# Sample sequences' state products interleaved with the output projection of one step

## What is computed

```python
def _gla_chunk(S, q, k, v, g):
    b = jnp.cumsum(g, axis=2)
    b_last = b[:, :, -1, :]
    o_inter = jnp.einsum('nhld,nhde->nhle', q * jnp.exp(b), S)
    ...
    o_intra = jnp.einsum('nhij,nhje->nhie', scores, v)
    k_dec = k * jnp.exp(b_last[:, :, None, :] - b)
    S_new = jnp.exp(b_last)[..., None] * S + jnp.einsum('nhld,nhle->nhde', k_dec, v)
    return S_new, o_inter + o_intra

def _layer(x, p, S0, conv_prefix, lw):
    h = _rmsnorm(x, lw['g_mix_pre'])
    proj = h @ lw['w_in']
    ...
    mix = jnp.concatenate([o, s_out], axis=-1) @ lw['w_out']
    x = x + _rmsnorm(mix, lw['g_mix_post'])
    ...
```

## Time and profile before

| | us |
|---|---|
| median of 3 runs | 2683.9 |
| lowest and highest run | 2680.67, 2685.6 |
| profiled execution | 2687.82 |
| its span in the trace | 2686.1 |
| PE busy in the span | 2605.3 (97%) |
| DVE, ACT, POOL busy | 1042.8, 878.9, 494.4 |
| mean granted clock of PE | 0.979 |

### The profile page before, as it was taken

The page is one execution under the profiler, slowest core; times in us unless marked ns, Lnnn a source line. Parts: engine busy times, 40 slices in busy tenths (PEclk is TensorE's granted clock), DMA queues, the critical chain, the costliest instruction groups (busy, mean ns, idle before and its releaser), DMA issues. The chain is left out here.

```text
span 2686.1 us, 36949 instructions
## 1 busy us (share of the span) xinstructions
PE 2605.3 (97%) x13668; PEld 2340.0 (87%) x13668; DVE 1042.8 (39%) x1721; ACT 878.9 (33%) x1796; POOL 494.4 (18%) x608
## 2 busy tenths in 40 slices
PE   8999999889999999999999999999899999999998
PEld 6789899768777899999999999999688878887887
DVE  4200000277884644444444444443511243334332
ACT  4311111243553533333333333333412142233322
POOL 1100100144654111111111111111000013231222
PEclk9999999878999999999999999999899999999999
DMA  5211222453344311111111111112644486653221
GB/s 169 86 63 61 71 71 66 130 155 108 109 134 142 124 54 41 53 40 54 38 57 38 57 37 58 35 57 74 186 112 107 112 246 174 197 155 116 70 88 44
DMA packets 269574, 254.35 MB, mean 95 GB/s; under 512 B 22792, under 2 KB 229356, under 8 KB 269452
## 3 DMA queue, kind: packets, MB, share of 16 engines
q1 hardware_dynamic: 269490, 253.24, 30.9%
HBM read 176.73 MB, written 76.46 MB: 94 GB/s over the span
## 5 line engine op out<-in xcount | busy, mean ns | idle before, releaser
L2132 PE MATMUL up_acc<-xh,up_wh 128*128 128x416 f32 x1760 | 619.6, 352 | 0.0
L2132 PE MATMUL up_acc<-xl,up_wh 128*128 128x416 f32 x1760 | 616.5, 350 | 0.0
L2132 PE MATMUL up_acc<-xh,up_wl 128*128 128x416 f32 x1760 | 616.1, 350 | 0.0
L2063 DVE SCALAR_TENSOR_TENSOR up_conv<-up_up,ffn_features,up_conv 128x416 f32<-128x416 f32 (+1 forms) x440 | 284.0, 646 | 570.1 <-ACT up_conv L1985 557.9
L2132 PEld LDWEIGHTS up_acc<-xh,up_wl 128*128 128x128 f32 x1760 | 330.1, 188 | 4.2
L2132 PEld LDWEIGHTS up_acc<-xl,up_wh 128*128 128x128 f32 x1760 | 330.8, 188 | 2.8
L2132 PEld LDWEIGHTS up_acc<-xh,up_wh 128*128 128x128 f32 x1760 | 329.9, 187 | 2.9
L1979 ACT ACTIVATE up_up<-up_acc 128x416 f32<-128x416 f32 (+1 forms) x220 | 113.0, 514 | 606.5 <-PE up_acc L2132 606.5
L2665 PE MATMUL down_acc<-ple_wh,ple_sh 128*128 128x512 f32 x704 | 276.8, 393 | 16.0 <-DVE ple_wl L2487 11.4
L2665 PE MATMUL down_acc<-ple_wl,ple_sh 128*128 128x512 f32 x704 | 276.2, 392 | 0.0
L2665 PE MATMUL down_acc<-ple_wh,ple_sl 128*128 128x512 f32 x704 | 275.8, 392 | 0.0
(11 more groups left out here) (337 smaller groups left out, 4234.4 us busy)
## 6 DMA issues: line engine op xcount, KB each, us to landing
lanes<-hidden SPq DMA_DIRECT2D x31, 1408.0 KB, 7.5
hidden<-up_conv SPq DMA_DIRECT2D x110, 208.0 KB, 1.9
up_raw<-in_w_up SPq DMA_DIRECT2D x44, 512.0 KB, 3.9
proj_features<-in_outs SPq DMA_DIRECT2D x60, 208.0 KB, 1.9
up_x_area<-in_w_down SPq DMA_DIRECT2D x40, 256.0 KB, 5.5
in_raw<-in_w_in SPq DMA_DIRECT2D x17, 512.0 KB, 4.0
in_x<-in_x_prompt SPq DMA_DIRECT2D x16, 512.0 KB, 3.6
mix_ru<-proj_features SPq DMA_DIRECT2D x16, 512.0 KB, 5.5
```

Of the source, the lines that this page charges most:

```text
L2063: last = nc.vector.scalar_tensor_tensor(out=out, in0=x(c), in1=out, scalar=taps[:, at, c:c + 1].rearrange("p a c -> p (a c)"), op0=ALU.mul ...
L2132: last = nc.tensor.matmul(acc[b][:, 0:TB], w[kind][:, k, :], x[:, k, b * TB:(b + 1) * TB], start=(k == 0 and p == 0), stop=(k == KC - 1 an ...
```

## The change

The 36 sample products of `sample_outputs` in step 6 are no longer issued in a row ahead of `make_kv(6)`. They keep their order and are issued one or two at a time (one after the first product, two after the second, and so on) behind the 24 products of half 1 of `project(4, 1)`. The waits stay ahead of the first of them. `mix_crossed(6)` still stands between the two pieces of half 1. `s_outputs` is signalled by the last sample product, now behind the last product of half 1.

```diff
-            def project(o, h, chunks):
+            def project(o, h, chunks, beside=None):
...
                     for p, (xx, ww) in enumerate(((sh, wh), (sh, wl), (sl, wh))):
                         last = nc.tensor.matmul(acc_of(o)[h][:, :], xx[s][:, k, :], ww[:, k, 512 * h:512 * h + 512],
                                                 start=(k == 0 and p == 0), stop=(k == KC - 1 and p == 2))
+                        if beside is not None:
+                            beside(k * 3 + p)
                 if k == KC - 1:
                     last.then_inc(summed, 1)
...
-            def sample_outputs():
-                pe.wait_ge(s_masked, 2)
-                pe.wait_ge(s_k_copied, 2)
-                pe.wait_ge(s_state_in, 32)
-                pe.wait_ge(s_v_in, 32)
-                for q in range(2):
-                    for f in range(2):
-                        h = 2 * q + f
-                        nc.tensor.matmul(s_o[f][:, q * TS:(q + 1) * TS], x.v[head_rows(f), h * DV:(h + 1) * DV],
-                                         x.scores[head_rows(f), q, :], start=True, stop=False)
-                        for b in range(SEQS):
-                            cols = slice(b * SL, (b + 1) * SL)
-                            last = nc.tensor.matmul(s_o[f][:, q * TS + b * SL:q * TS + (b + 1) * SL],
-                                                    x.state[head_rows(f), b, q, :], x.q_state[head_rows(f), q, cols],
-                                                    start=False, stop=(b == SEQS - 1))
-                last.then_inc(s_outputs, 1)
+            def sample_output(i):
+                q, f, b = i // 18, i // 9 % 2, i % 9 - 1
+                h = 2 * q + f
+                if i == 0:
+                    pe.wait_ge(s_masked, 2)
+                    pe.wait_ge(s_k_copied, 2)
+                    pe.wait_ge(s_state_in, 32)
+                    pe.wait_ge(s_v_in, 32)
+                if b < 0:
+                    nc.tensor.matmul(s_o[f][:, q * TS:(q + 1) * TS], x.v[head_rows(f), h * DV:(h + 1) * DV],
+                                     x.scores[head_rows(f), q, :], start=True, stop=False)
+                else:
+                    cols = slice(b * SL, (b + 1) * SL)
+                    last = nc.tensor.matmul(s_o[f][:, q * TS + b * SL:q * TS + (b + 1) * SL],
+                                            x.state[head_rows(f), b, q, :], x.q_state[head_rows(f), q, cols],
+                                            start=False, stop=(b == SEQS - 1))
+                    if i == 35:
+                        last.then_inc(s_outputs, 1)
+
+            def sample_outputs_beside(j):
+                for i in range(j * 3 // 2, (j + 1) * 3 // 2):
+                    sample_output(i)
...
                 if t == SB + 4:
                     sample_positions()
-                    sample_outputs()
...
                 if projects(t - 2):
-                    project(t - 2, 1, range(0, 4))
+                    project(t - 2, 1, range(0, 4), sample_outputs_beside if t == SB + 4 else None)
                 if mixes(t):
                     mix_crossed(t)
                 if projects(t - 2):
-                    project(t - 2, 1, range(4, KC))
+                    project(t - 2, 1, range(4, KC), sample_outputs_beside if t == SB + 4 else None)
```

## The result

The changed kernel is slower: 2701.67 us (median of 4 runs, 2697.98 to 2704.51) against 2683.3 of the kernel before on the same chip (4 runs, 2680.67 to 2685.6). The ratio is 1.0067, with an interval of 1.0055 to 1.008. On the medians that is +18.4 us; the forecast was +18.9.

The account below looks back on a forecast made before the run. PE, busy 97% of the span, was taken to bound the kernel. Step 6 +14.4, step 7's opening +2.0 and project(5, 0) +2.5 made +18.9 us, on the 2683.9 median 2703; range 2697 to 2708, low end widened to 2686.

Parts of the forecast that it names:

- The trips: Half 1 of step 6: 24 switches between 128-row and 64-row products expose weight loads, 0.3 us each at full clock, 0.43 at half.
- loads hide: Rival: in half 1 first passes load weights under the running product, no trip cost, clock holds; 2677 us, chance 0.07.
- the wait: End of step 6: mix_last waits for advance(6, 0), behind sample_copies on DVE, which waits for the last sample product; 1.3 us.
- The clock: Half 1: about 4 us at full clock, then 0.50 until some us into project(5, 0), about 40 us instead of 17.
- Step 6: Whole step after the change: 11.1 + 33 + 2.0 + 1.3 = 47.4 us against 33.0, +14.4.
- Up to half 1: Part of step 6 ahead of half 1: 11.1 us at full clock, with 1.1 of sample_positions.
- the groups: Half 1: one product, three passes on average and a trip take 0.87 us at full clock, 1.50 at half.
- Behind it: After step 6: step 7's slow opening +2.0 us and project(5, 0) at half clock +2.5.
- The opening: Step 7's first small products: 2.3 us before, about 4.3 at half clock, +2.0.
- The recovery: Start of project(5, 0) in step 7: runs at half clock until full clock is granted again, +2.5 us.
- `scale_rows(4)`: Step 7, ahead of project(5, 0): DVE is late, 5.8 us, but PE is ready only after 7.0 at half clock; no cost.
- Later steps move as a block: Steps after step 7 stay bound by PE as before and only shift, adding nothing.

Follow-up runs that it names:

- third experiment: Changed kernel with each of the 24 projection products of half 1 issued three times ahead of its sample products; 2698.88 us, ratio 1.0053 to the kernel before.
- the version with both heads: Changed kernel with both heads in one 128-row sample product, 20 products instead of 36, behind most of half 1's first 18 products; 2675.21 us, ratio 0.9974.
- the two kernels with both heads in a row: The both-heads version with its 20 products in a row behind sample_positions, 2677.03 us; and that with sample_state moved to the end of step 6, 2676.43 us.
- second and third experiment: Second: changed kernel with sample products of 128 rows instead of 64, padded with zeros, same places; 2683.44 us, ratio 1.0001. The third experiment has its own line.

## Why the prediction was right

**The trips.** The loads don't start under the products when the row count changes: 0.3 us per group at full clock, as forecast (0.86 in the third experiment against 0.87), and gone with the same row count (0.57). The rival "loads hide" is out for 64 rows. For 128 rows its mechanism is there, but not its price: the rival let the first pass of a group go free (0.23 + 2 x 0.11 = 0.45), and with the load hidden the group still takes 0.57. The Trainium skill (TensorEngine Tiling (Array Packing), "Key Properties") says that a change of the tiling mode drains TensorE; that is the rule that spoke against this change, and the loads at 659.20 and 660.87 agree with it. The rule behind the rival (weight loads are pulled ahead) held here only where the number of rows stayed. At half clock the trip was sized a little too high: 0.38 for the 0.43 assumed, so half the clock makes a trip only about a quarter dearer (0.30 at full clock). By these numbers, as an estimate, the 24 trips are 9 of the 14.7 us of step 6, the wait 1.3, and what is left is mainly the longer half clock.

**The clock.** Forecast: about 4 us at full clock in half 1, then 0.50 to some us into project(5, 0), about 40 us. Measured: 2.7 us, then 41.0. The reason given, too little projection in PE's stream, is supported by two comparisons. The 128-row kernels with 1.5 and with 2 sample products per group differ only in density (a product once in 0.57 or in 0.68 us); the first held 1.00 through half 1, the second fell to 0.50, in one profiled execution each. The stronger one is three products per trip, with the 64-row passes and all trips in place: it holds the clock through half 1 where one product per trip does not, and the means of all eight runs agree. From 652.97 to the wait of 1.32 ahead of 685.84 PE was busy all the time, at 0.50, so the absence of gaps did not save the clock.

**Step 6.** 47.7 against 47.4. Up to half 1 650.29 - 639.17 = 11.1 (11.1); the groups a little cheaper (1.45 for 1.50) but the full clock shorter; the wait 1.32 (1.3). Errors of some tenths cancelled each other, so the fit of the sum is better than that of its terms.

**Behind it.** Forecast +4.5, measured +3.3. The opening took 691.24 - 686.88 = 4.36 us (4.3). The recovery was sized too long: project(5, 0) ran 2.7 us at half clock, which loses 1.4, not 2.5. `scale_rows(4)` made PE wait no longer than before, as forecast, but the margin of 1.2 us was used up: DVE's `sample_k_seq` took 3.67 us and not the 2.59 of the earlier trace rows, with POOL active beside it:

```profile
686.64 3.67 DVE L1683 TENSOR_TENSOR sample_k_seq<-sample_k_tok,mc_own_seq 32x512 f32<-32x512 f32 x4
690.34 1.41 DVE L1594 SCALAR_TENSOR_TENSOR mix_y<-mix_out_acc,mix_rstd,mix_gain_rows 128x512 f32<-128x512 f32 x2
```

The first half of `mix_y` was there at about 691.1, and PE was ready at 691.24. Had the clock held, this would have been a wait, as it was in the version with both heads.

**What was missed.** "Later steps move as a block" was not right: step 8 lost its wait of 0.95 us, because the new delay moved two operations of DVE and POOL apart. Together with the recovery, that is why the spans differ by 16.7 and not by 18.9. That the medians differ by 18.4, only 0.5 from the forecast, is luck: the four runs of the changed kernel alone are spread over 6.5 us.

**What stays open.** Why the clock falls at one moment and not another: the two kernels with both heads in a row have the same PE program and were at 0.50 for 6.8 and 13.65 us. And what brought the clock down at the end of step 6 in the second and third experiment, the wait at `mix_last` or the passes that stand right up to it; the small products of step 7's opening come only after the fall. A version in which DVE's copies of the samples' result stand behind `advance` was not tried.

## What to carry to other kernels

Before small products are slipped between large ones, compare the row counts: a change of rows costs a drained load in each direction (0.3 us per trip here, more than the 0.23 of the product that was to cover it), while padding to the same rows with zeros did away with that (0.57 for 0.87 per group). It is not free everywhere: in a row it cost 3.75 us here. A PE that is never idle can still lose its clock among small products, so read the granted clock of the stretch and not only the busy share, and reduce the loads (both heads through one set of weights, 40 passes for 72: -7.8 us) before rearranging them. And when a signal moves behind the work that covered it, look who takes the place of the cover: `mix_last` waited 1.3 us here.

## What the runs showed of the hardware that was not expected

- 48 products more did not make the kernel slower than the changed one (2698.88 against 2701.67 us), with the clock at 1.00 through half 1.
- A POOL operation on one column took 1.40 us instead of 0.19 while a DVE operation of 128 x 2048 with two inputs ran, and ended with it. DVE suffers as well: `sample_k_seq` took 3.67 us instead of the 2.59 of the earlier trace rows. Three of its four operations took 0.67 and 0.68; the last took 1.75 (from 688.55), starting under a POOL operation of 1.47 (from 688.29). The Trainium skill (GPSIMD Engine Reference, "Specifications") says that the two share their SBUF interfaces and contend when DVE has two SBUF inputs; the trace agrees.
- The same products in a row lost the clock for 6.8 us in one kernel and 13.65 in another with the same PE program.
- A trip from 128 rows to 64 and back cost 0.30 us at full clock and 0.38 at half, while the passes and the products took twice as long at half (0.11 and 0.21, 0.23 and 0.43).
